# The last stage of a decoder step: a loop written out, its first sums begun from zero, its joins moved, its norm taken in token halves

## The reference, cut to what matters

```python
def rmsnorm(x, g):
    y = x * lax.rsqrt(jnp.mean(x * x, axis=-1, keepdims=True) + NORM_EPS)
    return y * g

def peer_block(xb):                       # e: chosen experts, gate: softmax of their scores
    h = jax.nn.gelu(einsum('bhkd,bd->bhk', peer_u[e], xb))
    return einsum('bhk,bhkd->bd', gate * h, peer_v[e])

x = x + peer(rmsnorm(x, norm2), ...)
return rmsnorm(x, norm_f)
```

## Time and profile before

| | us |
|---|---|
| median of 3 runs | 6010.47 (6008.94 to 6013.24) |
| the profiled execution | 6014.48 |
| its span | 6012.7 |
| TensorE busy | 5804.8 (97%), 48611 matmuls |
| VectorE busy | 3745.5 (62%) |
| ScalarE busy | 2424.2 (40%) |
| TensorE's mean granted clock | 0.984 of full speed |

### The profile page before, as it was taken

How to read it: one execution, slowest core, us unless ns; L and a number is a source line. 1 busy time by engine, 2 the same in 40 slices (tenths; PEclk the granted TensorE clock), 3 DMA queues, 4 the chain that set the end, 5 groups by cost and what they waited for, 6 DMA issues and landing times. The chain is left out here.

```text
span 6012.7 us, 116094 instructions
## 1 busy us (share of the span) xinstructions
PE 5804.8 (97%) x48611; PEld 5642.8 (94%) x48611; DVE 3745.5 (62%) x4760; ACT 2424.2 (40%) x3056; POOL 360.9 (6%) x249
## 2 busy tenths in 40 slices
PE   7999999999999999989999999999989999999997
PEld 7888889999999999989999999999989999999997
DVE  5565652323247533257876687777768888788787
ACT  3332322222223322122234443333336666666664
POOL 0000000000000000000036640000000000000000
PEclk9999999999999999999999999999999999999999
DMA  3111112322224433222234443333355454554541
GB/s 100 42 45 44 43 40 108 107 85 107 92 92 131 154 126 135 94 96 70 102 111 165 172 147 126 116 121 124 122 173 153 131 163 124 140 163 123 154 144 56
DMA packets 374432, 682.37 MB, mean 113 GB/s; under 512 B 222688, under 2 KB 233952, under 8 KB 346464
## 3 DMA queue, kind: packets, MB, share of 16 engines
q1 hardware_dynamic: 366928, 656.82, 33.5%
q10 hardware_dynamic: 7056, 19.00, 0.8%
HBM read 562.37 MB, written 113.37 MB: 112 GB/s over the span
## 5 line engine op out<-in xcount | busy, mean ns | idle before, releaser
L2700 PE MATMUL ps<-va_h_high,va_v_high 128*128 128x288 f32 x3584 | 1066.7, 298 | 44.8 <-issue 23.8
L2702 PE MATMUL ps<-va_h_high,va_v_low 128*128 128x288 f32 x3584 | 1062.5, 296 | 0.0
L2701 PE MATMUL ps<-va_h_low,va_v_high 128*128 128x288 f32 x3584 | 1061.5, 296 | 0.0
L2700 PEld LDWEIGHTS ps<-va_h_high,va_v_high 128*128 128x128 f32 x3584 | 678.5, 189 | 52.4 <-issue 25.2
L2701 PEld LDWEIGHTS ps<-va_h_low,va_v_high 128*128 128x128 f32 x3584 | 678.5, 189 | 0.1
L2702 PEld LDWEIGHTS ps<-va_h_high,va_v_low 128*128 128x128 f32 x3584 | 678.2, 189 | 0.0
L140 DVE TENSOR_TENSOR ah_ul<-ah_u,ah_uh 128x1024 fp32r<-128x1024 f32 (+1 forms) x288 | 428.9, 1489 | 264.3 <-ACT ah_uh L2256 212.7
L1145 PE MATMUL ps<-rwkv_hn_high,rwkv_wh 128*128 128x288 f32 x1664 | 493.8, 312 | 7.1 <-PEq L225 7.1
L140 DVE TENSOR_TENSOR rwkv_wl<-ret_w,rwkv_wh 128x2048 fp32r<-128x2048 f32 (+1 forms) x138 | 260.8, 1890 | 369.6 <-ACT rwkv_wh L1246 305.7
L1146 PE MATMUL ps<-hn_low,rwkv_wh 128*128 128x288 f32 x1664 | 471.3, 298 | 0.0
L2082 PE MATMUL ps<-hn_high,ah_uh 128*128 128x288 f32 x1536 | 431.5, 297 | 4.9 <-DVE ah_ul L140 4.8
(11 more groups left out here) (488 smaller groups left out, 14801.7 us busy)
## 6 DMA issues: line engine op xcount, KB each, us to landing
va_v<-peer_v SPq DMA_DIRECT2D x192, 512.0 KB, 5.5
ah_u<-peer_u SPq DMA_DIRECT2D x160, 512.0 KB, 4.7
ah_u<-peer_u SPq DMA_DIRECT2D x48, 1024.0 KB, 5.1
ret_w<-w_ret SPq DMA_DIRECT2D x47, 1024.0 KB, 4.8
h_kept<-ah_h SPq DMA_DIRECT2D x128, 288.0 KB, 2.2
gates<-ah_stage SPq DMA_DIRECT2D x12, 3072.0 KB, 9.6
va_h<-h_kept SPq DMA_DIRECT2D x128, 288.0 KB, 3.9
va_g<-gates SPq DMA_DIRECT2D x128, 288.0 KB, 5.6
```

The costliest lines, as they stand in the source:

```text
L2700: pe.matmul(z, ah[:, r, f], th[:, q, r, :], start=begin, stop=False, skip_group_check=True)
L2701: pe.matmul(z, ah[:, r, f], tl[:, q, r, :], start=False, stop=False, skip_group_check=True)
L2702: done = pe.matmul(z, al[:, r, f], th[:, q, r, :], start=False, stop=r == R - 1, skip_group_check=True)
```

## The change

1. The loops of the last stage are gone: SyncE, TensorE, ScalarE and VectorE have all 16 groups as straight code, and every semaphore's target is a constant.
2. In the first group P1, P7 and P6 begin from zero in the banks (`FROM_ZERO`): TensorE's first matmul of each bank has `start=True`, ScalarE copies nothing back, and VectorE copies where it added. GpSimd's clears and TensorE's six matmuls with ones in front are gone.
3. The last P4 no longer begins from zero: ScalarE copies its sum back into the banks, and VectorE joins only its own part (k = 1) of it.
4. The join of C11 stands in the last P6 and that of P1 with P6 in the last P3; the others follow in another order, the finished C22 and C12 each told apart, and the last four sums partly between them.
5. C12 is squared in four parts. TensorE sums the squares of the second half of the tokens (quarters 3 and 1) and then of the first (0 and 2), each with its own mean, Ln and Exp. VectorE scales 32 pieces of 288 tokens in place, second half first, and SyncE stores four pieces at a time, in rows of 1152 bytes.

```diff
+        FROM_ZERO = (P1, P7, P6)
+        LAST = 7 * (2 * TURNS - 1)
+        NORMED = (1, 3, 0, 2)
+        C11_JOINED, C22_JOINED, FIRST_BANKS, C12_JOINED, OTHER_BANKS, MEANS = 1, 2, 3, 4, 5, 8
 # SyncE
-            with sp.Fori(0, TURNS - 1) as d:
-                group(2 * d, True)
-                group(2 * d + 1, True)
-            group(2 * TURNS - 2, False)
-            for c in range(0, DC, 2):
-                sp.wait_ge(normed, c + 2)
-                sp.dma_start(out[:, c:c + 2, :], y[:, c:c + 2, :]).then_inc(stored, 16)
+            for g_ in range(2 * TURNS - 1):
+                group(g_, g_ < 2 * TURNS - 2)
+            for n, quarter in enumerate(NORMED):
+                t = slice(HT * (quarter % 2), HT * (quarter % 2) + HT)
+                for c in range(0, KD, 4):
+                    sp.wait_ge(normed, KD * n + c + 4)
+                    to = KD * (quarter // 2) + c
+                    sp.dma_start(out[:, to:to + 4, t], finals[:, quarter, c:c + 4, :]).then_inc(stored, 16)
 # GpSimd and TensorE
-            for to in (acc[P1], acc[P7], acc[P6]):
-                last = pool.memset(to, 0.0)
-            pe.wait_ge(zeroed, 3)
-            for k in BY_ACT:
-                for h in range(2):
-                    pe.matmul(pair(k)[:, h, :], K.ones[:, :], acc[P1][:, h, :], start=True, stop=True)
-                fresh = last and i == P4
+                fresh = entry and i in FROM_ZERO
-            with pe.Fori(0, TURNS - 1) as d:
-                for half in range(2):
-                    group(d, half, False)
-            group(TURNS - 1, 0, False)
-            group(TURNS - 1, 1, True)
-            pe.wait_ge(squared, 7)
-            for h, n in ((1, 1), (0, 0), (1, 2), (0, 3)):
+            for g_ in range(2 * TURNS):
+                for i in ORDER:
+                    product(7 * g_ + i, (g_ + i) % 2, i, g_ == 0)
+            pe.wait_ge(joined, FIRST_BANKS)
+            summed_squares(3, (2,), True, False)
+            summed_squares(1, (3, 4, 5, 6), False, True).then_inc(total, 1)
+            summed_squares(0, (1,), True, False)
+            summed_squares(2, (7, 8, 9, 10), False, True).then_inc(total, 1)
 # ScalarE, in swap
-                    if again:
+                    if not (entry and nxt in (P7, P6)):
 # VectorE, in the last group's products
+                elif i == P6:
+                    dve.wait_ge(swapped, 3 * (LAST + P2) + 6)
+                    join(C11, C11, acc[P1]).then_inc(joined, 1)
+                elif i == P3 and last:
+                    dve.wait_ge(swapped, 3 * (LAST + P6) + 6)
+                    join(acc[P1], acc[P1], acc[P6])
 # VectorE, behind them
+            join(C21, C21, acc[P1])
+            join(C22, C21, acc[P5]).then_inc(joined, 1)
+            join(C12, C12, acc[P1])
+            last_product(0)
+            dve.wait_ge(swapped, 3 * (LAST + P3) + 6)
+            join(C12, C12, acc[P3]).then_inc(joined, 1)
+            join(part(C21, BY_DVE), part(C21, BY_DVE), part(acc[P4], BY_DVE))
+            for k in range(1, 4):
+                last_product(k)
...
+            mean(0, 1)
+            for n, h in enumerate((1, 0)):
+                dve.wait_ge(rooted, n + 1)
+                for quarter in NORMED[2 * n:2 * n + 2]:
+                    for c in range(KD):
+                        f = KD * (quarter // 2) + c
+                        dve.scalar_tensor_tensor(out=finals[:, quarter, c, :], in0=finals[:, quarter, c, :],
+                                                 scalar=gain[:, f:f + 1], in1=rstd[:, HT * h:HT * h + HT],
+                                                 op0=ALU.mult, op1=ALU.mult).then_inc(normed, 1)
+                        if quarter == NORMED[1] and c == KD // 2 - 1:
+                            mean(1, 0)
```

More of the change, by code:

```diff
@@ L2579, in finish_stage @@
         block = ctx.enter_context(nc.Block())
-        def every_two(eng, two):
-            with eng.Fori(1, TURNS - 1) as d:
-                two(d, False, False)
         @block.sync
@@ L2783, in product @@
                         high(nxt, m + 1, ahead, r)
-                    swap(m, i, not (last and i == P3), entry)
+                    swap(m, i, entry)
             def two(d, first, last):
@@ L2795, in _ @@
                 act.copy(th[:, 0, r, :], b11[:, r, :]).then_inc(b_high, 1)
[L2796 to L2808 removed]
+            for d in range(TURNS):
+                two(d, d == 0, d == TURNS - 1)
+            act.wait_ge(joined, C11_JOINED)
+            act.activation(squares[:, 0], C11, ACT.Square).then_inc(squared, 1)
+            act.wait_ge(joined, C22_JOINED)
+            act.activation(squares[:, 3], C22, ACT.Square).then_inc(squared, 1)
+            act.wait_ge(joined, C12_JOINED)
+            for k in range(4):
+                act.activation(part(squares[:, 1], k), part(C12, k), ACT.Square).then_inc(squared, 1)
+            for k in range(4):
+                act.wait_ge(joined, OTHER_BANKS + k - 1 if k else FIRST_BANKS)
+                act.activation(part(squares[:, 2], k), part(C21, k), ACT.Square).then_inc(squared, 1)
+            for n, h in enumerate((1, 0)):
+                t = slice(HT * h, HT * h + HT)
+                act.wait_ge(joined, MEANS + n)
+                act.activation(rstd[:, t], rstd[:, t], ACT.Ln)
+                act.drain()
+                act.activation(rstd[:, t], rstd[:, t], ACT.Exp, scale=-0.5).then_inc(rooted, 1)
         @block.vector
@@ L2839, in sum_of, with add, join @@
                 dve.drain()
-            def add(m, i):
+            def add(m, i, fresh):
                 dve.wait_ge(made, 4 * m + BY_DVE + 1)
-                dve.tensor_tensor(part(acc[i], BY_DVE), part(acc[i], BY_DVE), pair(BY_DVE), ALU.add).then_inc(added, 1)
+                own = part(acc[i], BY_DVE)
+                if fresh:
+                    dve.tensor_copy(own, pair(BY_DVE)).then_inc(added, 1)
+                else:
+                    dve.tensor_tensor(own, own, pair(BY_DVE), ALU.add).then_inc(added, 1)
+            def join(to, one, other):
+                dve.drain()
+                return dve.tensor_tensor(to, one, other, ALU.add)
             def product(d, half, i, entry, last):
@@ L2911, in two @@
                         product(d, half, i, first and half == 0, last and half == 1)
-            def join(to, one, other):
-                dve.drain()
-                dve.tensor_tensor(to, one, other, ALU.add)
             for r in range(R):
@@ L2936, in _ @@
-            join(C12, C12, acc[P1])
-            dve.wait_ge(swapped, 3 * (M + P3) + 6)
-            dve.drain()
-            dve.tensor_tensor(C12, C12, acc[P3], ALU.add).then_inc(joined, 1)
-            for k in range(4):
-                dve.wait_ge(made, 4 * (M + P4) + k + 1)
-                dve.tensor_tensor(part(C21, k), part(C21, k), pair(k), ALU.add).then_inc(joined, 1)
-            dve.wait_ge(total, 1)
-            dve.tensor_scalar(halves(rstd[:, :]), SUM, 1.0 / D, EPS, ALU.mult, ALU.add).then_inc(joined, 1)
@@ L2945, in _, with last_product @@
-            dve.wait_ge(squared, 8)
-            for c in range(DC):
-                dve.scalar_tensor_tensor(out=halves(y[:, c, :]), in0=finals[:, 2 * (c // KD):2 * (c // KD) + 2, c % KD, :],
-                                         scalar=gain[:, c:c + 1], in1=halves(rstd[:, :]),
-                                         op0=ALU.mult, op1=ALU.mult).then_inc(normed, 1)
+            for d in range(TURNS):
+                two(d, d == 0, d == TURNS - 1)
+            def last_product(k):
+                dve.wait_ge(made, 4 * (LAST + P4) + k + 1)
+                dve.tensor_tensor(part(C21, k), part(C21, k), pair(k), ALU.add).then_inc(joined, 1)
```

56 lines of the change are left out of this document (19 added, 37 removed).

## The result

| | before | after |
|---|---|---|
| median, us | 6010.47 (6008.94 to 6013.24) | 5950.75 (5950.24 to 5954.5) |
| the profiled execution, us | 6014.48 | 5950.39 |
| its span, us | 6012.7 | 5948.6 |
| TensorE's mean granted clock | 0.984 | 0.988 |

The ratio is 0.990, with a 95% interval of 0.9889 to 0.9911: faster by 59.7 us.

A forecast was written before the change was run, and what follows sets the result against it. TensorE, busy 97% of the span, was taken as the bound, so only its standing or half-clock time could be won: 32.5 + 0 + 19.6 = 52.1 us off 6010.47 gives 5958.4, stated as 5959 us, range 5951 to 5977.

The forecast's parts named there:

- Term 1: Last stage's loops written out: groups 1 to 13 take 13 x 90.14 = 1171.8 us instead of 1204.3, gain 32.5 us.
- The upper bound of 42 us: Most the written-out loops could gain: groups 1 to 13 at 89.4 us each, as in a stretch where TensorE never stood.
- Term 2: Start of the last stage, without clears and matmuls with ones: gain 0 us, bounds -1 and +1.5 us.
- Term 3: End of the last stage, from joins through squares, sums and scalings to stores: gain 19.6 us, bounds 12 and 23 us.
- the rival of half clock: At the end, TensorE's sums restart at half clock after idling, ending some 1.7 us later; within a rival given 0.13.
- rival 4: At each group's start, the wait for VectorE's sum also goes: 9 us more gained, 5950 us; chance 0.06.
- 1 (the end set by something else): At the end, half-clock sums or 1152-byte stores falling behind VectorE set the time: 5966 or 5970 us; chance 0.13.
- 2 and 3 (straight code pays): Written-out groups keep part of the loop's price (5970 or 5981 us; chance 0.11), or starve for instructions (6031 us; 0.04).

The follow-up runs named there:

- e1: The kernel before with only its four loops (TensorE, ScalarE, VectorE, SyncE) written out, start and end as before: 5973.63 us, ratio 0.9943.
- e7: The changed kernel with VectorE's sum of P4 put ahead of the last two of four gate weighings, groups 0 to 14: 5938.67 us, ratio 0.9879.
- e2: The kernel before with only TensorE's loop written out, the other engines keeping theirs: 5982.3 us, ratio 0.9955.
- e3: The kernel before with the loops of ScalarE, VectorE and SyncE written out and TensorE's kept: 6005.14 us, ratio 0.9993.
- e6: The changed kernel with the old start put back (GpSimd's clears, matmuls with ones, ScalarE's copies ahead of P7 and P6): 5949.09 us, ratio 0.9895.
- the second profile of after: The changed kernel run once more, unchanged, for another profile: 5948.0 us in one run.
- e10: e7 plus C21's join moved earlier in the last product, x1's first quarter on its own semaphore and P2's pair added earlier in group 0: 5935.96 us, ratio 0.9877.
- e4: The kernel before with TensorE's loop of seven turns replaced by seven loops of one turn each: 5983.83 us, ratio 0.9958.
- e9: The kernel before with only the new start, TensorE's turn 0 written out and its loop over turns 1 to 6: 5996.77 us, ratio 0.9976.

## Why the prediction fell short, by its steps

**Term 1 (32.5 us) was the step that failed: the mechanism right, its size 3.0 us too small.** The straight groups took 1168.4 to 1168.8 us in all four profiles that have the loops written out and the old order of sums, where the term had 1171.8. The 13 groups gained 35.5 us (1204.3 to 1168.8), e1 alone 35.9. The working multiplied the distance from group 14 to group 15 of the kernel before, 90.14 us. I took it as straight code's own. But VectorE, ScalarE and SyncE leave their loops about there, and VectorE's sum came late: TensorE waited 0.74 us, against 0.47 us at every group of the kernel after. e1 shows straight groups at 89.87. Thirteen times 0.27 us is 3.5 us, which covers it. (The upper bound of 42 us was no bound either: e7's 13 groups took 1159.2 us, 45 us less than before.) The trace before had the number: at group 15, a whole group behind the loops' end, the wait was the shorter one; I used the distance between the two starts, which holds the longer. The parts of the term: TensorE's own jumps 26.6 us (e2), the other engines' loops 6.5 us beside the jumps (e3) and 9.3 to 9.4 us once the jumps are gone (e2 against e1).

**Term 2 (0 us) held within the scatter**, by e6 and by the second profile of after (123.17 us to group 1, as before); a gain under 1 us would not show, and lies within the term's bounds. The reason given held too: the third product waits for x1's last quarter, which ScalarE's copy waits for, in every profile but e10's.

**Term 3 (19.6 us) was right**: 19.9 us in the first profiles. Step by step: sums begin 1.17 us after the last product (1.3 said), first scaling 5930.22 - 5918.14 = 12.1 us after it (12.35), 0.435 us a scaling (0.434), 5948.6 - 5918.14 = 30.5 us from the last product to the end of the span (30.75). The granted clock was 1.00 behind the wait of 1.17 us, so the rival of half clock there did not come.

**The base.** What the terms leave, 59.7 - (35.5 + 0 + 19.9) = 4.3 us, is more than term 1's 3.0 us and belongs to no step of the sum (3.0, 0.3 and 4.3 make the 7.6 us that were missing). In the first profiles 2.6 us stand at the start and 6.1 in untouched stages, in the second 0.05 and 4.0. The untouched stages scatter by 11 us between profiles, and the kernel before itself had medians of 6007.9 to 6012.2 us beside the experiments. That the 4.3 us are such scatter is the likely reading; no run shows it. The sum from its median (5958.4) with the right size of term 1 gives 5955, within the range; that the time fell just outside took the scatter too. A range that ended at 5951 left 7 us below that sum for the scatter and for term 1's error together, while the terms' own bounds (42, 1.5 and 23 us) would have allowed 5944. I cut the range's lower end by the chance I gave rival 4, not by those bounds.

**The rivals.** 1 (the end set by something else): no, the stores kept 335 GB/s and more in the slices that they filled, and the sums full clock. 2 and 3 (straight code pays): no, 1078.80 us of groups at clock 1.00. 4 (the wait for the sum goes too): it does not go by itself, 7.1 us of it stayed; e7 shows that it needs another order.

## What to carry to other kernels

Where a turn of a TensorE loop is so long that its code is fetched again (1344 matmuls here), count the jump back at the wait and at the slow matmuls behind it; write such a loop out. Look first for a packet of instructions in the wait: the loops of 288 and 387 matmuls a turn were not fetched again, and lost nothing that shows. The bookkeeping of a loop costs TensorE nothing that shows either. Take the unit time of straight code from more than one sample, and not from the first piece behind another engine's loop. An accumulation that another engine waits for belongs ahead of work that nobody waits for yet; and where untouched stages scatter by more than the effect, compare stretches between fixed points instead of totals.

## What the runs showed of the hardware

**The clock behind a wait.** TensorE's granted clock takes two levels here (1.2 and 2.4 GHz). Ahead of the third product and at the groups' starts, long waits were followed by matmuls at the lower one and short waits were not. Between starts: 0.77 to 1.95 us, at most 2 slow starts in any profile; 2.10 us, 2 in e4 and 15 in e9; 2.40 us and more, 11 to 16 in the third product. So the length of the wait alone does not settle it: at 2.10 us it went both ways. The Trainium skill ("TensorE: Matmul & The Clock Gate", "Part 1: The HAM clock gate") says that an array that was idle starts again at half rate; the profiles agree for the long waits (granted clock 0.50 behind the 2.40 us of the second profile of after). With the matmuls with ones at the start removed the first product had 14 to 23 slow starts in place of 0 or 1, as feared in term 2, and it cost nothing that shows, since the second product waits longer anyway.

**Fetching.** A jump back of TensorE over 1344 matmuls left 3.7 to 4.9 us between starts in every profile that has it, with one packet of instructions landing in the wait; jumps back over 288 and 387 matmuls in the same program left 0.22 and 0.68 us, and their turns were not fetched again (one packet in 393 us, none in 195).
